# Feed-forwards of a two-block fp32 network: seven-product chunks from 10 to 16 per stage, the down product in two parts

## What is computed

```python
def swiglu(h, w1, w3, w2):                 # D_FF = 2816, four times in block one
    return (jax.nn.silu(h @ w1) * (h @ w3)) @ w2
def half_ffn(x, g, w1, w3, w2):
    return x + FFN_RES * swiglu(rmsnorm(x, g), w1, w3, w2)
def swiglu_2(h, w_gate_up, w_down):        # D_FF_2 = 2816, twice in block two
    g, u = jnp.split(h @ w_gate_up, 2, axis=-1)
    return (jax.nn.silu(g) * u) @ w_down
# block two, per layer:
    h = rmsnorm_2(x, norm2_w[l]) * (1.0 + sc2) + sh2
    x = x + g2 * swiglu_2(h, w_gate_up[l], w_down[l])
```

## Time and profile before

| | us |
|---|---|
| three runs, median (lowest, highest) | 3154.97 (3154.47, 3155.27) |
| the profiled execution's own time | 3154.14 |
| its span, first to last instruction | 3152.2 |
| TensorE busy | 3132.3 (99%) |
| TensorE weight load busy | 2618.7 (83%) |
| VectorE busy | 2013.7 (64%) |
| ScalarE busy | 1236.3 (39%) |
| GpSimd busy | 157.8 (5%) |

### The profile page before, as it was taken

How to read it: one execution, slowest core, us unless ns; L and a number is a source line. 1 busy time by engine, 2 the same in 40 slices (tenths; PEclk the granted TensorE clock), 3 DMA queues, 4 the chain that set the end, 5 groups by cost and what they waited for, 6 DMA issues and landing times.

```text
span 3152.2 us, 38120 instructions
## 1 busy us (share of the span) xinstructions
PE 3132.3 (99%) x15408; PEld 2618.7 (83%) x15408; DVE 2013.7 (64%) x2925; ACT 1236.3 (39%) x1812; POOL 157.8 (5%) x170
## 2 busy tenths in 40 slices
PE   9999999999999999999999999999999999999999
PEld 7888878888888888888888888887898888779887
DVE  5567567446856467557644685988893368889532
ACT  5322264322233222264332223565453235745321
POOL 2000000000000000000000000122000002300000
PEclk9999999999999999999999999999999999999999
DMA  5345322334542345432232463221233332022322
GB/s 151 97 131 190 124 84 94 94 96 145 190 137 81 94 133 181 140 94 81 86 102 94 147 192 117 82 70 41 78 111 104 100 87 84 28 80 95 120 87 74
DMA packets 334341, 339.92 MB, mean 108 GB/s; under 512 B 12502, under 2 KB 329208, under 8 KB 334168
## 3 DMA queue, kind: packets, MB, share of 16 engines
q1 hardware_dynamic: 332144, 333.80, 33.4%
q0 software_dynamic: 1792, 3.62, 0.4%
q10 hardware_dynamic: 232, 0.06, 0.0%
HBM read 335.36 MB, written 2.10 MB: 107 GB/s over the span
## 4 chain that ended last, share of the span: by engine, by line
PE 91%; DVE 5%; ACT 3%; issue 1%; DMA 0%; SPq 0%; DVEq 0%; ACTq 0%
PE ps L138 89%; PE ps L141 2%; ACT ar L95 1%; DVE wl L100 1%; DVE ar L100 1%; DVE ar L108 1%; ACT wh L95 1%; DVE ul L100 0%; ACT L95 0%; DVE T L108 0%; DVE hl L108 0%; ACT T L95 0%; ACT sp L95 0%; DMA ar<-in_x 0%; DVE T L100 0%
## 5 line engine op out<-in xcount | busy, mean ns | idle before, releaser
L138 PE MATMUL ps<-hh,wl 128*128 128x512 f32 (+1 forms) x2680 | 1026.4, 383 | 4.6 <-DVE wl L100 4.5
L100 DVE TENSOR_TENSOR wl<-raw,wh 128x1024 fp32r<-128x1024 f32 (+3 forms) x649 | 700.6, 1081 | 500.6 <-ACT wh L95 499.0
L138 PE MATMUL ps<-hh,wh 128*128 128x512 f32 (+1 forms) x2680 | 1019.2, 380 | 0.0
L138 PE MATMUL ps<-hl,wh 128*128 128x512 f32 (+1 forms) x2680 | 1019.0, 380 | 0.0
L95 ACT ACTIVATE wh<-raw 128x1024 fp32r<-128x1024 f32 (+3 forms) x649 | 602.5, 936 | 507.7 <-PE ps L138 462.0
L138 PEld LDWEIGHTS ps<-hh,wl 128*128 128x128 f32 x2680 | 504.8, 188 | 105.7 <-issue 11.0
L138 PEld LDWEIGHTS ps<-hh,wh 128*128 128x128 f32 x2680 | 505.0, 188 | 96.6
L138 PEld LDWEIGHTS ps<-hl,wh 128*128 128x128 f32 x2680 | 505.2, 189 | 93.2 <-issue 0.2
L138 PE MATMUL ps<-ul,wh 128*128 128x512 f32 (+1 forms) x1472 | 531.6, 366 | 0.0
L138 PE MATMUL ps<-uh,wl 128*128 128x512 f32 (+1 forms) x1376 | 503.7, 366 | 6.2 <-DVE wl L100 5.1
L138 PE MATMUL ps<-uh,wh 128*128 128x512 f32 (+1 forms) x1376 | 502.2, 365 | 0.0
(11 more groups left out here) (257 smaller groups left out, 2791.3 us busy)
## 6 DMA issues: line engine op xcount, KB each, us to landing
raw<-in_ffn_w SPq DMA_DIRECT2D x119, 1024.0 KB, 5.3
raw<-in_w_ada SPq DMA_DIRECT2D x48, 1024.0 KB, 5.2
raw<-in_w_gate_up SPq DMA_DIRECT2D x44, 1024.0 KB, 5.1
raw<-in_m_w_in SPq DMA_DIRECT2D x26, 1024.0 KB, 5.4
raw<-in_w_down SPq DMA_DIRECT2D x16, 1024.0 KB, 5.1
raw<-in_ffn_w SPq DMA_DIRECT2D x16, 768.0 KB, 4.3
raw<-in_w_in SPq DMA_DIRECT2D x12, 1024.0 KB, 5.3
raw<-in_m_w_out SPq DMA_DIRECT2D x8, 1024.0 KB, 5.2
```

The costliest lines, as they stand in the source:

```text
L100: return self.issue(lambda e: e.tensor_tensor(out, a, b, op))
L138: return self.issue(lambda e: e.matmul(out, l, r, start=start, stop=stop, skip_group_check=True))
```

## The change

Of `rounds`, the sets and the new functions:

```diff
-WOVEN = {s: {(w, j) for j in range(2, 7) for w in ("w1", "w3")} if s[0] == "ffn2" else set() for s in FFNS}
+WOVEN = {s: ({("w3", 2), *((w, j) for j in range(3, 11) for w in ("w1", "w3"))} - {("w3", 10)}) if s[0] == "ffn2" else set() for s in FFNS}
...
+def parts_of(s):
+    if WOVEN[s]:
+        return (range(0, 7), ((0, 8), (8, 6))), (range(7, 11), ((14, 8),))
+    return (range(0, 11), ((0, 8), (8, 8), (16, 6))),
...
+    for js, ks in parts_of(s):
+        for j in js:
...
+        for m in range(4):
+            for k in ks:
+                for a in range(2):
+                    yield "out", k, 2 * m + a, (k == ks[0]) + 2 * (k == ks[-1]) + 4 * (ks[-1][0] + ks[-1][1] == FT)
+                    if left:
+                        yield from rest()
+                        left = None
...
         diff_h = uh[:, 14:22, :].rearrange("p a n -> p (a n)").rearrange(quads, c=4, k=4)
-        diff_l = ul[:, 14:22, :].rearrange("p a n -> p (a n)").rearrange(quads, c=4, k=4)
+        diff_l = ul[:, 6:14, :].rearrange("p a n -> p (a n)").rearrange(quads, c=4, k=4)
...
-                if s[0] == "ffn":
-                    dve.tt(T3[a][:, :], ps((s, "w3", t))[:, :], R[:, :], MUL).then_inc(left((s, "w3", t)), (s, "w3", t))
-                    dve.own()
-                    silu_done(s, t)
-                    dve.tt(T3[a][:, :], T3[a][:, :], T1[a][:, :], MUL).then_inc(worked, (s, "gv", t))
...
+                silu_done(s, t)
+                dve.tt(T3[a][:, :], ps((s, "w3", t))[:, :], T1[a][:, :], MUL).then_inc(worked, (s, "gv", t))
...
             def differences(s):
-                for h in range(2):
-                    r = slice(4 * h, 4 * h + 4)
-                    for t in range(4 * h, 4 * h + 4):
+                if s != STAGES[0]:
+                    yield 1
+                for q in range(4):
+                    r = slice(2 * q, 2 * q + 2)
+                    for t in (2 * q, 2 * q + 1):
                         dve.wait_ge(hi_part, (s, "h", t))
                         dve.wait_ge(lo_part, (s, "h", t))
-                    dve.tt(full[:, r, :], hh[:, r, :].bitcast(F32), hl[:, r, :].bitcast(F32), ADD).then_inc(worked, (s, "full", h))
-                yield 1
+                    dve.tt(full[:, r, :], hh[:, r, :].bitcast(F32), hl[:, r, :].bitcast(F32), ADD).then_inc(worked, (s, "full", q))
+                    if q % 2:
+                        yield 1
...
+            def added(s, nxt, t, p):
+
+                dve.wait_ge(used, end_run(s, t, p))
+                b = ps((s, "o", p & 4, t))
+                key = (x_new, (s, t)) if p & 4 else (worked, (s, "first", t))
+                if s[0] == "ffn":
+                    dve.tt(T1[t % 2][:, :], b[:, :], R[:, :], MUL).then_inc(worked, (s, "turned", p & 4, t))
+                    x_free(s, t)
+                    dve.own()
+                    dve.stt(x[:, t, :], T1[t % 2][:, :], 0.5, x[:, t, :], MUL, ADD).then_inc(*key)
+                    return
...
-                        dve.ts(adab[:, 0:256], src[:, 0, :], c_act[:, 0:1], MUL).then_inc(worked, ("ada", i, 0))
...
+                        sums = adab[:, 0:256], adab[:, 256:512]
+                        for t in range(2):
+                            dve.ts(sums[t], src[:, t, :], c_act[:, t:t + 1], MUL).then_inc(worked, ("ada", i, t))
+                        for t in range(2, 8):
+                            dve.wait_ge(worked, ("ada", i, t - 2))
...
+                        dve.tt(sums[0], sums[0], sums[1], ADD).then_inc(worked, ("ada", i, 8))
```

More of the change, by code:

```diff
@@ L355, in build @@
+                if with_ada and (what, w, i) in ADA_AFTER[bool(WOVEN[key])]:
+                    plan_ada(1)
         for st in STAGES:
@@ L850, in woven_part, with out_run, emptied_by @@
                     banks.drop((s, "Y", w, j))
+            def out_run(s, nxt, k0, kt, t, p):
+                if p & 1 and t % 2 == 0:
+                    for c in (t, t + 1):
+                        banks.take((s, "o", p & 4, c), hold=True, freed=emptied_by(s, p, c))
+                b = ps((s, "o", p & 4, t))
+                g = G_of[(s, "w2", k0, t)]
+                step(g)
+                hi, lo = weights(g)
+                for k in range(kt):
+                    operand((s, "u"), k0 + k)
+                    done = pe.three(b[:, :], hi[:, k, :], lo[:, k, :], u_high(s, k0 + k), u_low(s, k0 + k),
+                                    p & 1 > 0 and k == 0, p & 2 > 0 and k == kt - 1)
+                done.then_inc(used, g)
+                pe.advance()
+                if p & 2:
+                    banks.drop((s, "o", p & 4, t))
+                if p & 6 == 6 and nxt is None:
+                    shown.append(t)
+            def emptied_by(s, p, t):
+                return (worked, (s, "turned", p & 4, t)) if s[0] == "ffn" else (x_new, (s, t)) if p & 4 else (worked, (s, "first", t))
             def ffn(s, nxt):
+                chain = None
                 for what, w, i, p in rounds(s):
@@ L1688, in ffn @@
                         later.append((w, 2 * i + p))
[L1689 to L1699 removed]
+                    elif what == "out":
+                        if nxt is None and p & 5 == 5 and i == 0:
+                            chain = act.beside(output())
+                        step(G_of[(s, "w2", w[0], i)])
+                        act.advance()
+                        while later:
+                            gated(s, *later.pop(0))
+                        if p & 6 == 6:
+                            after(nxt, i)
+                            if nxt is None:
+                                shown.append(i)
                 enter(nxt)
```

205 lines of the change are left out of this document (95 added, 110 removed).

## The result

| | before, us | after, us |
|---|---|---|
| median of four runs (lowest, highest) | 3154.90 (3154.47, 3155.27) | 3131.65 (3130.88, 3134.22) |
| the profiled execution's own time | 3154.14 | 3134.22 |
| its span | 3152.2 | 3132.4 |
| first ffn2 begins | 2207.96 | 2210.65 |
| first ffn2, length | 361.6 | 350.0 |

The ratio of the times is 0.9928, with a 95% interval of 0.9911 to 0.9945: 23.25 us less. The predicted time was 3131.6 us.

The account below looks back on a forecast made before the run. TensorE, busy 99%, bounds the kernel, with VectorE waits and slow clock at the ffn2 starts. Terms -9.8 - 14.2 + 0.3 + 0.3 = -23.4 us from 3154.14 give 3130.7; adjusted to the median, 3131.6 us, range 3126 to 3142.

Parts of the forecast that it names:

- Six more woven chunks per ffn2: In both ffn2 stages, 12 chunks go from 10.90 to 10.08 us, 0.82 us each: -9.8 us.
- Waits and slow clock at the starts: At both ffn2 starts, 10.9 us of TensorE waits and 3.3 us of slow clock all go: -14.2 us.
- the first rival: At the ffn2 starts, the differences still make VectorE late; half of the 14.2 us stays: 3138.7 us, chance 0.14.
- Joints: Where woven and plain chunks meet, two gaps per ffn2 instead of one, as a full buffer's split needs two halves: +0.3 us.
- The end: At the program's end, tile 5 is turned back there too, 12 transposes instead of 8: +0.3 us, bounds 0 and 1.
- `R`: In the ffn stages, 22 VectorE products go and 8 come per stage, none on the path: 0 us.
- The bound for lost cover: After each ffn, should VectorE's 4.4 us of idle cover before the sums be gone: 4 x 0.7 us.
- The prediction's own sign for this: It is wrong if the stages before the first ffn2 end over a microsecond away from 2208 us.
- `ada`, tile 12, tile 21: `ada` sums 0 (bounds -0.5, +0.5); tiles at the down product's two parts 0, covers 8 and 4.8 us.
- 6 us are free: Ahead of the first woven chunk, eight runs give 43.5 us for 37.2 us of VectorE work.
- decides from the point where the 5.2 us that VectorE idles in 60 are gone, 0.9 us more work per chunk: In the woven chunks, VectorE's limit starts to cost time only after 0.9 us more work per chunk.
- VectorE cannot hold the woven pace: Rival: each of 16 woven `w3` chunks waits 1.6 us and loses as much to the clock: 3183 us, chance 0.03.

Follow-up runs that it names:

- the run with ten: The changed kernel with ten woven chunks per ffn2 again instead of 16, all else as changed: 3141.72 us, ratio 0.9961.
- the run with one part: The kernel before with only its ten woven chunks moved one chunk later and the differences in small pieces; down product in one part: 3139.50 us, ratio 0.9954.
- large pieces: The changed kernel with `full` in two large operations one step earlier and everything behind them two steps earlier: 3138.94 us, ratio 0.9950.
- the two runs with seventeen: The changed kernel with `w1` 2 woven too, 17 chunks per ffn2: 3152.07 us; the same with `differences` begun one step earlier: 3145.42 us.
- `w3` 10 woven: The changed kernel with `w3` 10 woven too, its last two parts directly ahead of the second down product: 3134.67 us, ratio 0.9939.
- the small operation: The changed kernel with one more 128x128 VectorE operation in every woven chunk: 3140.01 us, ratio 0.9957.
- one more op: The changed kernel with one more 128x512 VectorE operation in every woven chunk: 3150.36 us, ratio 0.9989.
- three more operations: The changed kernel with three more 128x512 VectorE operations in every woven chunk: 3198.67 us, ratio 1.0143.
- the mix on GpSimd: The changed kernel with part 3's mix on GpSimd instead of VectorE: 3131.99 us; with one more 128x512 VectorE operation per woven chunk besides: 3147.34 us.

## Why the prediction was right

- **Time and sign.** 3131.6 was predicted, 3131.65 measured. The two ffn2 stages gave -22.5 us and the first and third ffn took +1.2, -21.3 together, where the sum had -23.4. The agreement of the medians to 0.05 us is luck: the stages gave 2 us less than the sum, and the medians lie 2 us further apart than the stages. A slow stretch of 1.6 us that some executions have and others have not (see the last section) is of that size.
- **Six more woven chunks per ffn2: -9.8.** Shown by the run with ten: 4.6 a stage, -9.2 us. A chunk is worth 0.77, not 0.82. The page after keeps the pitch (503 in 60 us) that the term was taken from. The estimate from the Trainium skill (TensorE: Matmul & The Clock Gate, "Back-to-back issue gap"), 14 us for both stages, is too high here; the page gives that formula for an isolated matmul.
- **Waits and slow clock at the starts: -14.2.** Shown by the run with one part: 7.0 us in the first ffn2. In the second it is 369.1 - 362.4 = 6.7 us with the end unchanged. Together -13.7. All of the waits of before went, not half, as the first rival had it, and the -13.7 already hold the new wait of 0.57 us in each stage. The two means were both needed: large pieces at their old place bring the first wait back, and the two runs with seventeen show that with small pieces a start one chunk earlier is too early.
- **Joints: +0.3.** Two parts against one part made no difference of a tenth in the first ffn2. The size was right and the reason was not: the gap stands ahead of part 6 of the row's last woven chunk, where by the leads VectorE's stock is used up, and not at the split of a full buffer for the plain chunk.
- **The end: +0.3.** 0.4 by the two runs with ten chunks.
- **`R`: 0, was +1.2.** This step failed. "None is on the path" counted the products that go, and the cover behind the last ffn. The eight that come stand in the down product, each between a finished output tile and the next split, and two of the four stages pay 0.6 us for it. The bound for lost cover, 4 x 0.7 us, was of the right size. The prediction's own sign for this, an ffn2 that begins more than 1 us from 2208, was there, though 1.6 of the 2.7 us are start-up.
- **`ada`, tile 12, tile 21: 0.** No wait stands at any of them. Even with `w3` 10 woven, so that tiles 20 and 21 come later still, the down product behind them did not wait.
- **What the sum lacked.** The 0.57 us wait for ScalarE's copy in the first woven chunk, once per stage. The kernels with ten chunks that start in this place have the same row.

Two further steps were argued wrongly, though nothing of the time hung on them.

- **"6 us are free".** The count of work against time was right in that nothing was late. It was no measure of the reserve: starting one chunk earlier brought one wait of 9.4 us, because the order is strict and the last piece stands behind work that TensorE needs later. A sum over runs cannot see that; the order at the piece that TensorE asks for first can.
- **VectorE "decides from the point where the 5.2 us that VectorE idles in 60 are gone, 0.9 us more work per chunk".** The 5.2 us were no room at all; VectorE is 0.12 us a chunk behind already, in before too (its turn there is 20.39 us, from 2313.38 to 2333.77), and the stock is what counts. It ends with the row of nine, so the point is reached with no more work at all, and the small operation, 0.32 us a chunk, is well past it. So the rival "VectorE cannot hold the woven pace" was right that VectorE is the slower one in these chunks. Its reason and size were not: VectorE does use for the next `w3` chunk what a `w1` chunk leaves free, and is short by 0.24 us a pair, not by 1.6. "Ten chunks in a row ran without such waits" was good evidence for rows of nine and seven, as the prediction used it, and for no longer ones. From its tenth chunk on a longer row would lose 0.12 us a chunk, some 0.8 us for a row of 16 (an estimate from the turns); that was not tried, nor whether the down product was put in between for it.

The best version is after with `R` and `ada` as before: 3130.64 us. By the medians it is the same as after; by the stages it is 1.2 us shorter.

## What to carry to other kernels

Idle time of an engine is no room if the engine waits for one that had waited for it: measure its turn, from one wait to the same wait of the next round, and set that against the pace of the engine it feeds. An engine that is a little too slow is hidden by what was made ahead, until the row of such work is long enough. When work must be ready for a first use, read the engine's order back from that use, and not only the sum of the work ahead of it.

## What was unexpected of the hardware

The granted clock also fell where TensorE had not waited. In the profiled execution of after it is (columns as in the earlier trace rows):

```profile
171.00:173.00 2.00, 2.00 (x12) 1.76 (x12) 1.16 (x7) 0.00 (x0) 0.00 (x0) 1.00 0.82 286
173.00:174.00 1.00, 1.00 (x4) 0.73 (x4) 0.93 (x4) 0.00 (x0) 0.00 (x0) 0.50 0.00 0
```

It is the lower of the two levels, 1.2 of 2.4 GHz, in the first ffn. Kernels with identical code there have it in one profiled execution and not in another: with the new `R` the first ffn took 359.1 us with it (after, ten woven) and 357.5 without (large pieces, one more op), with the old one 358.5 (before) and 356.9 (one part). So 1.6 us come and go with it. Where TensorE did wait, the fall did not follow in every case: during the 9.4 us of the early start it came, behind waits of 2.1 us in some places and not in others (not behind the first), with three more operations behind some waits of 2.3 to 2.8 us and not behind others, and behind the waits in the kernels with one more operation (up to 1.3 us, with the mix on GpSimd up to 1.7) or the small one (up to 0.9) it did not.

The other surprise is the price of GpSimd beside VectorE, above: a product of two `T` took 1.28 us instead of 0.69, although GpSimd's subtraction ran beside it for only 0.73 us (2303.19 to 2303.92); in that time it gained little more than 0.1 us. `T<-ps,sq`, which reads one of its inputs from PSUM and overlapped GpSimd's by 0.5 us, kept its 0.69. GpSimd's own 1.29 us did not grow by it: at 2431.66 us, with VectorE idle, the same operation took 1.28. The Trainium skill (GPSIMD Engine Reference, the row "SBUF interfaces" of its table of specifications) says that GpSimd shares them with VectorE, with contention where a VectorE instruction has two SBUF inputs; the rows agree, and they give the price.
